# Decoder step on one core: head sums inside the attention, a gather in three parts, sample tokens twice on partitions, down weights split to 16 bits

## Chip, cores and metric

One core of a Trainium2 chip runs the whole program. The metric is the device time of one execution in microseconds; time before is the median of three runs. A profiled execution gives the trace.

## What is computed

One inference step of a two-layer decoder for a prompt group (256 tokens) and a sample group (8 sequences of 8 tokens), D = 1024, all in float32; T = 320 tokens in all.

```
layer 0: x += W_out_a [mLSTM heads | gated short conv] (rmsnorm(x))
layer 1: x += W_out_c [rms_norm per head(diff_attention(rope(q), rope(k), v)) * subln_g * (1 - lam_init)]
         (8 heads of 128; prompt causal, samples over a paged cache of 256 positions)
both:    x += W_mem_o mem_attention(rmsnorm(x))       (4 heads over 256 memory tokens)
         x += MoE(rmsnorm(x)): 4 groups of 8 experts, top 1 group, top 2 experts in it;
              y = sum_e gate_e * W_down_e( silu(W_gate_e x) * (W_up_e x) ),  d_ff = 256
end:     rmsnorm(x)
outputs also: new states, keys and values of the step
```

## The kernel before, in words

**Projections.** Weights arrive in units of 256 columns on SP's queue, in the order of `STREAM`. ACT makes the high float16 part (`split_hi`, L539), DVE the low part (`split_lo`, L546), and PE multiplies in three float16 products (`mm3`, L552 to L554). The low part of a unit releases its landing buffer, for which SP waits. Activations are kept with features on partitions, tokens on the free axis.

**Attention** (`attend_pe`, `attend_act`, `attend_dve`; kind "d" is the differential one of layer 1, "m0" and "m1" the memory ones). Eight iterations, one sample sequence each; in "d" each has also a prompt unit `u` (64 queries, four heads). Per iteration PE does scores, key transposes (L1406), weight transposes (`weights_t`, L1433; `unit_t`, L1485) and mixes (L1445, L1501), ACT the exponentials and copies (the last of a unit is L1570, into `xn`), DVE maxima and factors.

**Norm of the heads** (`subln_*`), when all units are done: ACT squares all of `xn` (L1818), PE sums with a matrix of ones (L1812), ACT takes logarithm and exponential in halves (L1822, L1823; each change of function loads a table), DVE scales (L1832). Then `input_act` and `input_dve` split `xn` in two halves, and `gemm_pe("out_c")` starts.

**Routing** (`memo_pe`, `route_*`). Router logits are computed with tokens on partitions in three tiles of 128, 128 and 64 tokens (L641), between the units of the memory output projection, the last set behind it, as are the token sums (L656). PE transposes the normalized tokens (L1847), ACT and DVE split them to `xnh` and `xnl`, DVE picks the experts, PE ranks the tokens (L1853 to L1858), and DVE builds `pk`, a 0/1 matrix from tokens to 704 slots sorted by expert (128 slots first, 576 later). The largest count of an expert, ready at L1940, goes to `roff`; `moe` loads it on each engine and branches: experts with at most 64 tokens take the body with one round, which is the one that runs here.

**Experts** (`moe_*`). PE gathers expert inputs into `xg` by products of `xnh` and `xnl` with `pk` (`gather_first`, L2007: six products for each of nine chunks; last the gates, L2015; then it transposes the positions, L2020). POOL copies 64 slots of each of the pair's two experts to `xe` (L2236, L2250). PE multiplies in float32 with the gate and up weights (`up`, L2048), two 64-row halves of the array for the two experts, followed by `weigh`, whose end releases the gate and up buffer (`gu_used`). After the first pair's `up` comes the gather of the other 576 slots in two halves (L2034, 108 products of 288 columns), with copies by ACT (L2167) and DVE (L2197). Step q is: `up(q)`, `weigh(q)`, `select(q)` (L2070), `combine(q-2)` (L2092), `down(q-1)` in two halves (L2112, float32) around `transpose_h(q)` (L2121). DVE makes the hidden values (L2214 to L2219), ACT and DVE split the result to `yh` and `yl` (L2171, L2204), and DVE's last step there releases the down buffer (`dw_used`). In layer 1, `seed` (L2081) adds x into the output banks before the second pair.

**SP's queue for the experts** (L430, L439) is written out by hand: pairs 0 and 1 with their down weights and pair 2's gate and up weights (there are two buffers of each, so pair g waits for the release of pair g-2), then for each p the gate and up weights of p+1 and the down weights of p. One pair is 4 MB of gate and up and 2 MB of down weights, 16 pairs a layer.

## Time and profile before

| | |
|---|---|
| median of three runs | 1442.78 us (1439.38 to 1445.84) |
| profiled execution | 1440.08 us, span 1438.8 us |
| granted TensorE clock, mean | 0.939 |
| PE busy | 1276.6 us, 89% |
| DVE / ACT / POOL busy | 582.3 / 413.9 / 143.6 us |
| read from HBM, written | 328.21 MB, 10.54 MB |
| experts' stages | about 485 to 745 us and 1160 to 1426 us |
| differential attention | about 862 to 950 us |

The span is from the first to the last instruction; the execution's own time has some 1.3 us more around it. A busy share is an average over stages with different limits, so a stage is read by its own rows. In the timeline a row gives the start, the duration, engine, line, operation, output and inputs, how many instructions are merged, and in brackets how long the engine was idle before and what ended that.

### The profile page before, as it was taken

Reading aid. Unit: us, or ns where it says so; the run is one execution under the profiler, and the core shown is the slowest. Engines: PE = TensorE matmul, PEld = TensorE weight load, DVE = VectorE, ACT = ScalarE, POOL = GpSimd, SP = SyncE. Lnnn points to the kernel's source line nnn. Section 1 sums busy time; section 2 is a strip of 40 time slices with the busy share of each in tenths; the row PEclk is TensorE's granted clock in tenths of the full one; section 3 lists DMA queues with packets and bytes.
Section 4 is the critical chain, followed back from the end, with each engine's and each line's share of the span. In section 5 each row is a group of like instructions: output and inputs, shape, how many; then the busy total and the mean of one; then the engine's idle time right before and its main releaser. Section 6 shows DMA issues by size and latency. Waiting matters only on the chain.

```text
span 1438.8 us, 20890 instructions
## 1 busy us (share of the span) xinstructions
PE 1276.6 (89%) x8470; PEld 793.9 (55%) x8470; DVE 582.3 (40%) x1152; ACT 413.9 (29%) x729; POOL 143.6 (10%) x189
## 2 busy tenths in 40 slices
PE   6799999989889799989989979958897979999995
PEld 5676688866656543333337757735664755333332
DVE  3655367655434522211244665425433452121212
ACT  3443323254332211111144224444432311111112
POOL 5100031110001110100000230000000101010100
PEclk9799998799998799999999989988998979999998
DMA  8464353357638069999963567302963624999992
GB/s 243 153 210 123 116 164 114 109 180 282 246 119 359 3 248 421 421 421 421 421 219 118 194 203 267 114 0 88 319 239 149 283 89 187 421 421 420 421 422 112
DMA packets 112826, 340.22 MB, mean 236 GB/s; under 512 B 7486, under 2 KB 75402, under 8 KB 84048
## 3 DMA queue, kind: packets, MB, share of 16 engines
q1 hardware_dynamic: 107296, 322.20, 59.5%
q0 software_dynamic: 4992, 15.47, 3.4%
q8 instruction: 69, 1.13, 0.3%
q10 hardware_dynamic: 432, 1.11, 0.2%
q14 instruction: 37, 0.30, 0.1%
HBM read 328.21 MB, written 10.54 MB: 235 GB/s over the span
## 4 chain that ended last, share of the span: by engine, by line
PE 66%; DMA 19%; DVE 7%; ACT 3%; issue 3%; SPq 1%; POOL 1%; POOLq 0%; ACTq 0%; DVEq 0%
DMA arena<-in_w_exp_up 15%; PE ps L2048 11%; PE ps L552 8%; PE ps L553 8%; PE ps L554 8%; PE ps L2112 2%; PE ps L1445 2%; PE ps L1501 2%; PE ps L2034 2%; PE ps L2092 2%; PE ps L1420 2%; PE ps L1406 1%; PE ps L1485 1%; DVE wl L546 1%; DMA stg<-in_w_mem_k 1%
## 5 line engine op out<-in xcount | busy, mean ns | idle before, releaser
L2048 PE MATMUL ps<-arena,mkv 128*64 128x512 f32 x1024 | 230.1, 601 | 26.8 <-DMA arena<-in_w_exp_up 21.7
L552 PE MATMUL ps<-bx,wh 128*128 128x320 f16 (+1 forms) x640 | 195.3, 305 | 38.9 <-DVE bx L777 15.5
L546 DVE SCALAR_TENSOR_TENSOR wl<-stg,wh 128x1024 f16<-128x1024 f32 x128 | 160.8, 1295 | 98.3 <-ACT wh L539 98.3
L553 PE MATMUL ps<-bx,wh 128*128 128x320 f16 (+1 forms) x640 | 195.2, 305 | 0.0
L554 PE MATMUL ps<-bx,wl 128*128 128x320 f16 (+1 forms) x640 | 195.0, 305 | 0.0
L539 ACT ACTIVATE wh<-stg 128x1024 f16<-128x1024 f32 x128 | 128.4, 1050 | 180.3 <-PE ps L554 158.1
L2048 PEld LDWEIGHTS ps<-arena,mkv 128*64 128x64 f32 x1024 | 82.1, 138 | 170.3 <-issue 164.8
L2204 DVE TENSOR_TENSOR arena<-ps,arena 128x512 f16<-128x512 f32 x64 | 44.1, 689 | 143.2 <-ACT arena L2171 92.4
L552 PEld LDWEIGHTS ps<-bx,wh 128*128 128x128 f16 x640 | 65.2, 102 | 65.5 <-issue 34.7
L552 PE MATMUL ps<-arena,wh 128*128 128x320 f16 x288 | 87.7, 304 | 3.7 <-DVE arena L1368 3.0
L2208 DVE COPY arena<-ps 128x1 f32<-128x1 f32 x32 | 5.1, 158 | 211.5 <-PE ps L2070 211.5
L554 PE MATMUL ps<-arena,wl 128*128 128x320 f16 x288 | 87.6, 304 | 0.0
L553 PE MATMUL ps<-arena,wh 128*128 128x320 f16 x288 | 87.6, 304 | 0.0
L2171 ACT CAST arena<-ps 128x512 f16<-128x512 f32 x64 | 37.5, 586 | 166.0 <-PE ps L2112 166.0
L2092 PE MATMUL ps<-arena,rstd 128*128 128x512 f16 (+1 forms) x384 | 78.9, 384 | 5.7 <-DVE arena L2204 5.7
L553 PEld LDWEIGHTS ps<-bx,wh 128*128 128x128 f16 x640 | 64.8, 101 | 24.5 <-issue 1.5
L554 PEld LDWEIGHTS ps<-bx,wl 128*128 128x128 f16 x640 | 64.9, 101 | 24.0
L2250 POOL COPY mkv<-bx 128x576 f32 x60 | 40.1, 671 | 375.5 <-PE ps L2070 316.9
L2176 ACT ACTIVATE mkv<-ps 128x256 f32<-128x256 f32 x30 | 11.5, 384 | 221.9 <-PE ps L2048 221.9
L1406 PE MATMUL ps<-cst,arena 128*128 128x128 f32 x384 | 57.3, 284 | 12.1 <-DVE arena L1580 7.7
L2112 PE MATMUL ps<-arena,mkv 128*64 128x512 f32 x256 | 61.5, 598 | 0.0
L2112 PE MATMUL ps<-stg,mkv 128*64 128x512 f32 x256 | 60.6, 597 | 0.0
(414 smaller groups left out, 1849.1 us busy)
## 6 DMA issues: line engine op xcount, KB each, us to landing
arena<-in_w_exp_gate SPq DMA_DIRECT2D x64, 1024.0 KB, 15.1
arena<-in_w_exp_up SPq DMA_DIRECT2D x64, 1024.0 KB, 17.2
arena<-in_w_exp_down SPq DMA_DIRECT2D x32, 1024.0 KB, 17.7
stg<-in_w_exp_down SPq DMA_DIRECT2D x32, 1024.0 KB, 17.6
arena<-in_cache_mem_k SPq DMA_DIRECT2D x16, 1024.0 KB, 7.1
arena<-in_cache_mem_v SPq DMA_DIRECT2D x16, 1024.0 KB, 5.2
stg<-in_w_in_a SPq DMA_DIRECT2D x28, 512.0 KB, 4.7
stg<-in_w_qkv_c SPq DMA_DIRECT2D x20, 512.0 KB, 4.3
```

The lines of the kernel that those rows point to most:

```text
L539: nc.scalar.mul(wh[:, s, c], src[:, c], WSCALE).then_inc(S["w_hi"], 1)
L546: nc.vector.scalar_tensor_tensor(wl[:, s, c], src[:, c], WSCALE, wh[:, s, c], ALU.mult, ALU.subtract).then_inc(S["w_lo"], 1)
L552: nc.tensor.matmul(out, wh[:, s, at:at + 128], hi, start=start, stop=False)
L553: nc.tensor.matmul(out, wh[:, s, at:at + 128], lo, start=False, stop=False)
L554: return nc.tensor.matmul(out, wl[:, s, at:at + 128], hi, start=False, stop=stop)
L1406: last = nc.tensor.transpose(ps[:, TB[f % 2], 256 * i + 128 * t:256 * i + 128 * t + 128], kpg[:, b % 2, t, at:at + 128], ident)
L2048: last = nc.tensor.matmul(ps[64 * j:64 * j + 64, UB, :], xe[:, q % 2, j, k, :], gu[:, g % 2, j, :, k, :], start=(k == 0), stop=(k == KD - ...
L2092: last = nc.tensor.matmul(out, csel[:, q % 3, 128 * i:128 * i + n], y[:, 512 * half:512 * half + 512], start=(first and y is yh), stop=(fi ...
L2112: last = nc.tensor.matmul(ps[64 * j:64 * j + 64, (Y0, Y1)[half], :], hT[:, q % 2, 128 * kk + 64 * j:128 * kk + 64 * j + 64], dws[g % 2][:, ...
L2171: nc.scalar.copy(yh[:, 512 * half:512 * half + 512], ps[:, (Y0, Y1)[half], :]).then_inc(M["y_hi"], 1)
L2204: V.tensor_tensor(yl[:, f], ps[:, (Y0, Y1)[half], :], yh[:, f], ALU.subtract).then_inc(M["y_lo"], 1)
L2250: nc.gpsimd.tensor_copy(xe[:, q % 2, j], xg[:, :, ds(at, CAP)]).then_inc(M["xe_ready"], 1)
```

## The change

Four parts:

1. **Head sums in the attention.** ACT squares each prompt unit when it is mixed, PE sums it in the next iteration in front of `weights_t`, DVE copies the sums out in front of `unit_factors`; the sample tokens' squares come with the last unit. Behind the attention are left the logarithms, then root, scaling, high and low part by chunk pairs; the first unit of `out_c` takes the pairs as they come.
2. **Sample tokens twice on partitions** (`per_token`). The third tile's 64 tokens stand in both halves of the 128 partitions, by two products each in logits, sums and transposes. The upper half of `xnh`'s third tile holds the low part, so that a gather needs five products and not six.
3. **Gather in three parts** of 128, 128 and 448 slots. The first (`first_pe`, `first_act`) stands in front of the branch on PE and ACT, with the gates and the position transposes. Then `up(0)`, the second part, three chunks of the third, `up(1)`, and the other six chunks. `seed` comes after the first step's down products.
4. **Down weights of pairs 2 to 14** (`HALVED`) are split by ACT and DVE to `dnh` and `dnl` (`halve`); three float16 products replace one in float32, and `hT` is split as well (`hTl`, for which `up(q+1)` waits). The down buffer is released when DVE has made the low part.

```diff
+    def per_token(out, x, rhs, i, **flags):
+        if i < 2:
+            return nc.tensor.matmul(out, x[:, 128 * i:128 * i + 128], rhs, skip_group_check=True, **flags)
+        for half in range(2):
+            last = nc.tensor.matmul(out[64 * half:64 * half + 64], x[:, NP:T], rhs, skip_group_check=True, **flags)
+        return last
...
@@ attend_pe @@
+        def head_sum(u):
+            pe.wait_ge(S["hsq_ready"], HA + u + 1)
+            pe.wait_ge(S["ppv_ev"], u0 + u + 1)
+            nc.tensor.matmul(ps[:, PVB, 256:512], ones[:], sqd[:, u % 2, :], start=True, stop=True,
+                             skip_group_check=True).then_inc(S["hsum_ready"], 1)
...
+            if c["diff"] and i:
+                head_sum(i - 1)
             weights_t(i)
...
@@ attend_act @@
+                if c["diff"] and u == 7:
+                    act.wait_ge(S["bpv_ev"], b0 + 8)
+                    nc.scalar.activation(sqs, xn[:, :, NP:T], ACT.Square).then_inc(S["hsq_ready"], 1)
                 act.wait_ge(S["ppv_ps"], u0 + u + 1)
+                if c["diff"]:
+                    if u >= 2:
+                        act.wait_ge(S["hsum_ready"], u)
+                    nc.scalar.activation(sqd[:, u % 2, :], ps[:, PVB, 0:256], ACT.Square).then_inc(S["hsq_ready"], 1)
...
@@ attend_dve @@
             weights(i)
+            if c["diff"] and i:
+                head_sums(i - 1)
...
@@ subln_act @@
-        nc.scalar.activation(sq[:], xn[:], ACT.Square).then_inc(S["hsq_ready"], 1)
-        act.wait_ge(S["hsum_ready"], 2)
-        for half in range(2):
-            h = slice(4 * half, 4 * half + 4)
-            link(nc.scalar.activation(sq[:, h], ps[:, h, 0:T], ACT.Ln, bias=epsc[:, 0:1], scale=1.0 / 128))
-            nc.scalar.activation(sq[:, h], sq[:, h], ACT.Exp, scale=-0.5).then_inc(S["hstd_ready"], 1)
+        act.wait_ge(S["hsum_ev"], 7)
+        log(slice(0, 4), slice(0, NP), hsum[:, 0:4, 0:NP])
+        log(slice(4, 8), slice(0, 192), hsum[:, 4:8, 0:192])
+        act.wait_ge(S["hsum_ready"], 9)
+        log(slice(0, 8), slice(NP, T), ps[:, 2, :].rearrange("p (h t) -> p h t", h=KD))
+        act.wait_ge(S["hsum_ready"], 10)
+        link(log(slice(4, 8), slice(192, NP), ps[:, 3, 0:256].rearrange("p (h t) -> p h t", h=4)))
+        root(0)
+        root(1)
+        high(0)
+        root(2)
+        high(1)
+        root(3)
+        high(2)
+        high(3)
...
@@ moe_pe @@
+    PARTS = ((xnh, 0), (xnl, 0), (xnh, 1), (xnl, 1), (xnh, 2))
+    RBANK = (0, 1, 6, 2, 3, 4)
+    HALVED = range(2, NPAIR - 1)
...
+            if rounds == 1 and q in HALVED:
+                for kk in range(2):
+                    pe.wait_ge(S["dn_lo"], 4 * (len(HALVED) * l + q - HALVED[0]) + 2 * half + kk + 1)
+                    for n, (h, w) in enumerate(((hTh, dnh), (hTh, dnl), (hTl, dnh))):
+                        for j in range(2):
+                            at = 128 * kk + 64 * j
+                            last = nc.tensor.matmul(ps[64 * j:64 * j + 64, (Y0, Y1)[half], :], h[:, q % 2, at:at + 64],
+                                                    w[:, j, kk, f], start=(kk == 0 and n == 0),
+                                                    stop=(kk == 1 and n == 2), skip_group_check=True)
...
         if rounds == 1:
             up(0)
             weigh(0)
-        gather(0, 18)
-        select(0)
-        transpose_h(0)
-        if l == 1:
-            seed()
+            gather_next()
+            gather_rest(0, 3)
+            select(0)
+            transpose_h(0)
+            up(1)
+            weigh(1)
+            gather_rest(3, 9)
...
@@ moe_act @@
+        def halve(q):
+            g = NPAIR * l + q
+            act.wait_ge(dw_in[g % 2], 32 * (g // 2 + 1))
+            if q == HALVED[0]:
+                act.wait_ge(S["xg_ps"], 15 * l + 15)
+            for half in range(2):
+                f = slice(512 * half, 512 * half + 512)
+                if q - 1 in HALVED:
+                    act.wait_ge(M["y_ps"], 2 * q - 1 + half)
+                for kk in range(2):
+                    nc.scalar.mul(dnh[:, :, kk, f], dws[g % 2][:, :, kk, f], WSCALE).then_inc(S["dn_hi"], 1)
...
         for q in range(last_step + 1):
+            if rounds == 1 and q - 1 in HALVED:
+                halve(q - 1)
+            gate_half(q)
...
@@ pe_memory, act_memory @@
         route_pe(pe, l)
+        first_pe(pe, l)
         moe(pe, l, moe_pe)
```

## Rows read from the trace of the kernel before

**Rows 1.** The page, chain that ended last: shares by engine.

```profile
PE 66%; DMA 19%; DVE 7%; ACT 3%; issue 3%; SPq 1%; POOL 1%; POOLq 0%; ACTq 0%; DVEq 0%
DMA arena<-in_w_exp_up 15%; PE ps L2048 11%; PE ps L552 8%; PE ps L553 8%; PE ps L554 8%; PE ps L2112 2%; PE ps L1445 2%; PE ps L1501 2%; PE ps L2034 2%; PE ps L2092 2%; PE ps L1420 2%; PE ps L1406 1%; PE ps L1485 1%; DVE wl L546 1%; DMA stg<-in_w_mem_k 1%
```

**Rows 2.** Stretches: length, busy of PE, PEld, DVE, ACT, POOL; clock, DMA share, GB/s.

```profile
600.00:700.00 100.00, 92.50 (x462) 35.56 (x464) 19.45 (x47) 11.37 (x25) 9.36 (x14) 1.00 1.01 421
```

**Rows 3.** Timeline of PE, one step of the expert stage.

```profile
544.63 7.04 PE L2048 MATMUL ps<-arena,mkv 128*64 128x512 f32 x32
...
551.83 2.47 PE L2092 MATMUL ps<-arena,rstd 128*128 128x512 f16 x12
554.13 1.88 PE L2112 MATMUL ps<-arena,mkv 128*64 128x512 f32 x8
...
558.15 7.04 PE L2048 MATMUL ps<-arena,mkv 128*64 128x512 f32 x32
```

**Rows 4.** Timeline of SP's queue: pair 3's weights, layer 0, layer 1.

```profile
527.02 0.33 SPq L430 DMA_DIRECT2D arena<-in_w_exp_gate  x1
...
1208.09 0.33 SPq L430 DMA_DIRECT2D arena<-in_w_exp_gate  x1
```

**Rows 5.** Timeline around the branch and the first pairs, both layers; L2034: chain of waits.

```profile
480.66 0.14 DVE L1940 TENSOR_SCALAR roff<-arena 1x1 int32<-1x1 f32 x1
...
483.63 4.03 DVE L1959 SCALAR_TENSOR_TENSOR wl<-ps,rtok,wh 128x512 f16<-128x512 f32 x6
485.51 2.72 PE L2007 MATMUL ps<-arena,wh 128*128 128x128 f16 x24 [6.12 <-issue]
...
491.00 0.54 PE L2020 MATMUL ps<-cst,arena 128*32 128x128 f32 x3
...
493.92 8.78 PE L2048 MATMUL ps<-arena,mkv 128*64 128x512 f32 x32 [2.38 <-POOL mkv L2236]
...
502.76 13.35 PE ps L2034 x108
...
519.84 7.09 PE L2048 MATMUL ps<-arena,mkv 128*64 128x512 f32 x32 [0.51 <-POOL mkv L2250]
...
1169.20 8.79 PE L2048 MATMUL ps<-arena,mkv 128*64 128x512 f32 x32 [2.11 <-POOL mkv L2236]
...
1194.61 6.20 PE L2081 MATMUL ps<-cst,xT 128*128 128x128 f32 x45
```

**Rows 6.** Timeline, end of the differential attention and norm of the heads.

```profile
929.24 0.88 PE L1433 MATMUL ps<-arena,bx 128*128 128x64 f32 x6 [1.03 <-DVE arena L1591]
...
949.61 0.37 ACT L1570 COPY bx<-ps 128x256 f32<-128x256 f32 x1 [2.09 <-PE ps L1501]
...
952.43 1.28 ACT L1822 ACT_TABLE_LOAD   x1
952.46 7.47 PE L1812 MATMUL ps<-arena,ones 128*128 128x320 f32 x16 [2.89 <-ACT arena L1818]
...
964.00 1.55 DVE L1832 SCALAR_TENSOR_TENSOR bx<-bx,lams,arena 128x1280 f32<-128x1280 f32 x1 [16.48 <-ACT arena L1823]
...
975.45 0.44 PE L552 MATMUL ps<-bx,wh 128*128 128x320 f16 x1 [15.51 <-DVE bx L777]
```

**Rows 7.** Stretches as in rows 2, start of the output projection.

```profile
975.00:1001.00 26.00, 25.55 (x176) 17.89 (x177) 13.38 (x15) 10.61 (x15) 2.22 (x2) 0.93 0.27 84
```

**Rows 8.** Timeline of the routing in layer 0.

```profile
450.08 1.57 PE L641 MATMUL ps<-wrt,bx 128*128 128x36 f32 x12
...
473.24 4.69 PE L1847 MATMUL ps<-cst,bx 128*128 128x128 f32 x24
...
478.28 0.26 DVE L1922 TENSOR_TENSOR arena<-arena 128x96 bf16<-128x96 f32 x1
```

**Rows 9.** The page, groups: line, shapes, count, busy, mean ns, idle before.

```profile
L546 DVE SCALAR_TENSOR_TENSOR wl<-stg,wh 128x1024 f16<-128x1024 f32 x128 | 160.8, 1295 | 98.3 <-ACT wh L539 98.3
...
L539 ACT ACTIVATE wh<-stg 128x1024 f16<-128x1024 f32 x128 | 128.4, 1050 | 180.3 <-PE ps L554 158.1
```

More of the change, by code:

```diff
@@ L655, in memo_pe @@
             for c in (0, 1, 6, 7):
[L656 to L657 removed]
+                last = per_token(ps[:, 7, i:i + 1], sq[:, c, :], ones[:, 0:1], i, start=(c == 0 and i == 0),
+                                 stop=(c == 7))
         last.then_inc(S["sum_ready"], 1)
@@ new lines, in subln_pe @@
+        nc.tensor.matmul(ps[:, 2, :], ones[:], sqs.rearrange("p h t -> p (h t)"), start=True, stop=True
+                         ).then_inc(S["hsum_ready"], 1)
+        pe.wait_ge(S["hsq_ready"], HA + 9)
+        nc.tensor.matmul(ps[:, 3, 0:256], ones[:], sqd[:, 1, :], start=True, stop=True
+                         ).then_inc(S["hsum_ready"], 1)
+        u0, base = UNIT["out_c"][0], IN["out_c"][0]
+        pe.wait_ge(S["w_ev"], u0)
+        for p in range(4):
+            if p % 2 == 0:
+                pe.wait_ge(S["w_lo"], u0 * 2 + p // 2 + 1)
+            pe.wait_ge(S["in_lo"], base + p + 1)
+            last = unit_mm(0, T, xh, xl, ks=(2 * p, 2 * p + 1))
@@ new lines, in subln_pe, with log, root, high @@
+        last.then_inc(S["w_used"], 1)
+        gemm_pe(pe, "out_c", first=1)
+    def subln_act(act, link):
+        def log(h, t, src):
+            return nc.scalar.activation(hsum[:, h, t], src, ACT.Ln, bias=epsc[:, 0:1], scale=1.0 / 128)
+        def root(p):
+            k = slice(2 * p, 2 * p + 2)
+            nc.scalar.activation(hsum[:, k], hsum[:, k], ACT.Exp, scale=-0.5).then_inc(S["hstd_ready"], 1)
+        def high(p):
+            k = slice(2 * p, 2 * p + 2)
+            act.wait_ge(S["y_ready"], p + 2)
+            nc.scalar.copy(xh[:, k], xn[:, k]).then_inc(S["in_hi"], 1)
+        act.wait_ge(S["hsum_ev"], 7)
[13 more added lines that the diff above has]
+        high(3)
@@ L1837, in build @@
+        scaled(0)
+        scaled(1)
+        low(0)
+        scaled(2)
+        low(1)
+        scaled(3)
+        low(2)
+        low(3)
     NFIT = ROUNDS * NE
@@ new lines, in gather_rest @@
+        def gather_rest(k0, k1):
+            for k in range(k0, k1):
+                if k < 2:
+                    pe.wait_ge(S["xg_act"], 10 * l + k + 2)
+                elif k in (3, 4, 5):
+                    pe.wait_ge(S["xg_dve"] if k == 4 else S["xg_act"], 5 * l + 1 if k == 4 else 10 * l + 5)
+                elif k >= 6:
+                    pe.wait_ge(S["xg_dve"] if k % 2 else S["xg_act"], 5 * l + 2 if k % 2 else 10 * l + 6 + (k - 6) // 2)
+                for n, (x, i) in enumerate(PARTS):
+                    last = nc.tensor.matmul(ps[:, RBANK[k % 6], 0:SR], x[:, i, k, :], pk[:, i, S1:NSLOT],
+                                            start=(n == 0), stop=(n == 4))
@@ L2147, in moe_pe @@
             down(q - 1, 1)
+            if q == 1 and l == 1:
+                seed()
         combine(last_step - 1)
@@ L2151, in moe_pe, with first_act @@
         combine(last_step)
+    def first_act(act, l):
+        for b in range(3):
+            act.wait_ge(S["xg_ps"], 15 * l + b + 1)
+            dst = xg[:, 4 * b:4 * b + 4, 0:S0] if b < 2 else xg[:, KD, 0:S0]
+            src = ps[:, FIRST[b], :].rearrange("p (k c) -> p k c", k=4) if b < 2 else ps[:, FIRST[b], 0:S0]
+            nc.scalar.copy(dst, src).then_inc(S["xg_act"], 1)
     def moe_act(act, l, rounds):
```

372 lines of the change are left out of this document (213 added, 159 removed).

## The prediction

> **What bounds the kernel now.** I read the chain that ended last first. Products on PE hold most of it, and the one transfer in it is the experts' gate and up weights with 15% of the span [rows 1]. The question is where that transfer decides, so the stretch table came next: between 600 and 700 us the DMA engines move 421 GB/s, busy share 1.01 [rows 2]. A pair of experts brings 4 MB of gate and up and 2 MB of down weights, 6.29 MB, so 14.9 us at that rate. PE's own step is shorter, 13.5 us from one pair's up products to the next (544.63 to 558.15) [rows 3]. Both expert stages are therefore bound by the transfer, once it runs without a gap. What sets their end is when that gapless run begins. SP's queue says when: the up weights of pair 3 are issued at 527.02 and 1208.09 [rows 4], and from there all follows at 14.9 us a pair. The first up products start at 493.92 and 1169.2 [rows 5]. I call this point U: pair 3 is released at U+33.1 in layer 0 and U+38.9 in layer 1.
>
> The second place is the norm between the differential attention and its output projection. The last mix ends at 949.6, and the projection's first product starts at 975.45 [rows 6]: 25.8 us in which ACT, PE and DVE take turns.
>
> **1. Head sums in the attention.** Removed: one Square over 2560 elements, eight f32 sums (7.47 us), the four passes of logarithm and exponential with four table loads of 1.28 us, and the wait of all casts for both scalings (1.55 us each) [rows 6]. What is left behind the last mix, with durations scaled by elements: Square and copy 0.8, load 1.3, four logarithms (2560 elements, at the splits' 1.05 us per 1024 [rows 9], with starts) 2.8, load 1.3, first root 0.7, DVE's scaling 0.8, ACT's cast 0.65, DVE's remainder 0.75; sum 9.3 after 949.6, so the first product at 958.9. The other three chunk pairs come 1.4 to 1.6 us apart, and PE's 12 products for each take as long. The projection ran 176 products in 25.55 us at a granted clock of 0.93 [rows 7]: 0.135 us each at full speed and 1.8 us lost at the start. Before, its first unit of 48 products ends at 975.4+6.5+1.8=983.7. Now the first pair runs at half clock (3.2 us), the others at 1.6: 958.9+3.2+4.9=967.0. That is 16.7 us earlier; the units behind it follow their splits as before, and so does the wait for the memory output weights.
>
> Added in each of eight iterations: an f32 sum over 256 columns (0.53 us for 320, so 0.43), a Square on ACT (0.37), a DVE copy (0.4). The sum stands in front of the product that waits 1.03 us for DVE [rows 6], which covers it; the Square lies between the mix and the next exponentials, where ACT is idle. The DVE copy stands in front of the factors that the next weight transposes wait for, with about 0.2 us of cover. If all were covered, nothing; if all were serial, 1.2 us an iteration, 8.4 in seven. I take 1.6, since the longest of the three is inside a shown wait. Net 15.1.
>
> **2. The gather.** After U: up products of pair 0, 8.8 us [rows 5]. Then 45 products of 128 columns; 24 took 2.72 us at half clock [rows 5], so 2.5 in all at full speed (5 at the other). Then 15 of 448 columns, 0.19 each by the 2.30 us of 12 products [rows 3]: 2.8. Select, gate and transposes: before, 17.1 us between the end of up products and pair 1's (502.7 to 519.84) hold 13.4 of gather [rows 5], leaving 3.7; a last eviction is no longer waited for, so 3.3. Pair 1 starts at U+17.4 and releases pair 3's weights at U+24.6, 8.5 us sooner. The other 30 gather products (5.7), an eviction (0.7), pair 0's down products with the transposes (4.0 by 554.13 to 558.15 [rows 3]) and pair 2's up products (7.1) put the release of pair 4 at U+42.3. In between the queue runs dry for some us: pair 3's transfer ends at about U+36. So the gain is not 8.5: before, pair 4's turn came at U+33.1+14.9=U+48.0, now it comes at U+42.3, 5.7 sooner. In layer 1 the seed, 6.2 us for 45 records at a mixed clock [rows 5], moves from before pair 1 to before pair 2, and runs at about 4.8 there: U+47.1 against U+53.8, 6.7.
>
> **3. U itself moves.** Sample tokens twice on partitions means two 64-wide f32 products for one. Router logits: 12 records take 1.57 us [rows 8]; four more per call, three calls inside a PE-bound projection: 1.3. The sums and the last call: 8 records at 0.1 and 4 at 0.18: 1.6. The last eight of 24 transposes (4.69 us for all [rows 8]) become 32 records. No row has 64-wide f32 records of 128 columns; a quarter of the up products' 0.22 us is 0.054, the seed's average record is 0.138, and I take 0.08: 2.6 us. They would end at 480.6, half a us behind the expert mask (478.54 [rows 8] plus 1.6): 0.6 (0 to 2.5). DVE's route loses a memset and four split operations: minus 0.5. Sum 3.0.
>
> Then the branch. The count is ready at 480.80, and PE's first product behind its branch starts at 485.51, 6.1 idle, "issue", though DVE had its last operand at 483.6 and went on to the low parts [rows 5]: 4.7 us for load, compare and jump. It lies before the first gather now, where DVE's work on slots covers most of it. The change puts the branch behind the first gather and the position transposes, which end at 491.54 and would end at 494.5. So U goes from 493.92 to 498.7 (4.7, less 0.5 for a sequencer that runs ahead): 4.8 later. Expert inputs would be there sooner: DVE's low parts end at 487.66 plus 3, eight products 0.9, ACT's copy 0.6, POOL's load and copies 2.2: 494.3. If the jump were free, U moves 0.6.
>
> The Trainium skill (Runtime: NRT & Kernel Launch, Instruction fetch mechanics) says that a taken branch to code outside the fetched window stalls for a DMA fetch. By it the jump costs PE wherever it stands in the program, which speaks against the move: 4.2 us a layer that a free jump would not take. By that rule the sum is 1425, without it 1416.6. The idle time named "issue" agrees with it.
>
> Net: layer 0 5.7-4.8=0.9, layer 1 6.7-4.8=1.9.
>
> **4. Down weights split.** Before, 8 f32 products a pair: 4.0 us with transposes 0.4. After, 24 f16 products of 64 columns' width. In the combine, 8 wide ones and 4 of half width take 2.30 us [rows 3]; 8 at 0.213 leave 0.6, 0.15 each, so half-width ones overlap in twos. 24 take 2.6 to 3.6, I say 2.8: PE saves 0.8 a pair, and the step goes to about 12.8. Added: ACT four splits a pair (1.05 each), DVE four (1.30 each) [rows 9], DVE's low part of the hidden rows 0.4. DVE is then busy for 8.7 of 14.9 us, ACT 6.1. The splits wait for down weights, and ACT's tanh of the next pair is queued behind them: with the weights 5 us after the up weights, tanh comes at 9.6, the second half's split ends at 13.4 and the next up products may start at 14.6, just under 14.9. A step that misses this starts late once, and takes from no transfer, as weights are released 11 us before their turn. Worth nothing: the transfer hides it. The last pair isn't split, and combine(14) falls within 0.3 us of where it was.
>
> **Sum.** 15.1+0.9+1.9=17.9: the profiled 1438.8 (1440.08 with what lies around it) becomes 1420.9. It ran 2.7 below the median of 1442.78; from the median: 1424.9, say 1425.
>
> **Rivals.**
> - *The jump is hidden after all* (code fetched while PE waits for DVE). Against: "issue" in both layers. 4.2 us a layer: 1416.6. Chance 0.17.
> - *The attention pays in full*: the copy, sum and Square in series, 8.4 instead of 1.6: 1431.8. For it: the factors stand right behind the copy. Against: the 1.03 us wait in front of the sum. 0.15.
> - *Half-width f16 products don't overlap*: 24 at 0.213 are 5.1, step 15.3, 0.4 over the transfer in 26 steps: 1435. Against: the combine. 0.07.
> - *Slower: PE becomes the bound of the expert stage.* The same place, with each half-width product's weight load (0.05) uncovered too: 6.3 us, step 16.5, 1.6 in 26 steps: 1466. It decides from a step of 15.9, where the 17.9 and 7.2 us are used up. 0.06.
> - *The gather gives nothing and the transposes in the route run at 0.138*: 2.5 us more a layer and no earlier release: 1438. 0.05.
>
> The split does take effect: it stands in the one-round branch, and the 13.5 us steps are those of one round a pair.
>
> **How the numbers follow.** Forecast 0.50, its own range 1420 to 1431. 0.5% is 7.2 us, about what a measurement of this kernel can tell: faster below 1435.6. Faster: 0.50+0.17+0.15 and half of the third rival, 0.84; same 0.09; slower 0.07. The range 1414 to 1436 leaves out the slow case, the last and part of the noise.
>
> **What would show it.** The first projection product behind the attention 9 us after the last mix; iterations there up to 0.3 us longer; PE idle some 4.7 us with "issue" between position transposes and first up products; pair 3's weights issued 25 us after those, pair 4's at 42 and 47; 14.9 us a pair with 421 GB/s; a DVE row of splits at 1.3 us with no wait of PE on it. I would be wrong if the stretches fall below 421 GB/s, if the attention's iterations grow by a us, or if the jump isn't there.

## The result and the profile after

| | before | after |
|---|---|---|
| median | 1441.72 us (1439.38 to 1445.84, 4 runs) | 1422.27 us (1418.38 to 1424.52, 4 runs) |
| profiled execution, its span | 1440.08, 1438.8 | 1424.52, 1423.2 |
| PE, DVE, ACT busy | 1276.6, 582.3, 413.9 | 1260.6, 713.2, 511.3 |

The ratio is 0.9859 (95%: 0.9827 to 0.9891). It is faster, by 19 us where 17.9 were worked out, and 1422.3 lies inside the range and 3 us under the forecast. A second timing of the same kernel gave 1421.31 and a ratio of 0.9880 (0.9850 to 0.9911).

Where it went shows when the span is cut at instructions that both kernels have: the issue of the experts' first weights, the first staged loads of the next projection behind them, the loads of the second and third cached values, the loads of the next memory weights. In us, from one cut to the next:

| stretch | before | after | again | gain |
|---|---|---|---|---|
| start to experts' first weights, layer 0 | 430.33 | 432.94 | 424.24 | |
| layer 0's experts, to the projection's loads | 311.26 | 311.60 | 309.62 | -0.3, 1.6 |
| projection, to the cached values | 120.26 | 119.42 | 118.14 | |
| attention, norm, first output units | 124.46 | 108.01 | 108.10 | 16.4 |
| memory attention | 119.13 | 119.16 | 119.14 | 0 |
| layer 1's experts, to the end | 333.36 | 332.07 | 331.96 | 1.3, 1.4 |

So, by the stages of these profiles, one of the four parts carries the change: the head sums. The first stretch has the same code in all kernels and still differs by 8.7 us between two executions of one; that is the size of what one execution can't tell.

The end of the differential attention and its norm, timeline of after (start, length, engine, line, out<-in; in brackets the idle time before and who ended it):

```profile
949.45 2.00 PE L1522 MATMUL ps<-bx,arena 128*128 128x64 f32 x16 [0.45 <-ACT bx L1590]
...
952.15 1.28 ACT L1865 ACT_TABLE_LOAD   x1
...
953.45 1.97 ACT L1865 ACTIVATE mkv<-mkv,epsc 128x1024 f32<-128x1024 f32 x2
955.33 1.03 ACT L1865 ACTIVATE mkv<-ps,epsc 128x512 f32<-128x512 f32 x2
...
957.66 1.36 ACT L1869 ACTIVATE mkv<-mkv 128x640 f32<-128x640 f32 x2
958.54 1.68 DVE L1902 SCALAR_TENSOR_TENSOR bx<-bx,lams,mkv 128x640 f32<-128x640 f32 x2 [9.16 <-ACT mkv L1869]
959.46 0.72 ACT L1874 CAST bx<-bx 128x640 f16<-128x640 f32 x1 [0.43 <-DVE bx L1902]
...
961.19 0.43 PE L558 MATMUL ps<-bx,wh 128*128 128x320 f16 x1 [8.40 <-DVE bx L1908]
```

It answers to [rows 6]. The last mix ends at 951.45, the projection's first product starts at 961.19: 9.7 us, where before had 25.8. Behind the mix stand ACT's square and copy (0.7 us), a table load, four logarithms of 3.0 us in all, a second load, the first root, DVE's scaling and ACT's cast. PE's idle time falls from 15.51 to 8.40.

Then the branch and the first pairs. Timeline of after: DVE, PE and POOL in layer 0 (count ready, first gather, its gate part, position transposes, expert inputs, the up products of pairs 0 and 1), last row layer 1:

```profile
483.25 0.14 DVE L2021 TENSOR_SCALAR roff<-arena 1x1 int32<-1x1 f32 x1
...
486.61 1.87 PE L2083 MATMUL ps<-arena,wh 128*128 128x128 f16 x16 [4.41 <-DVE arena L2032]
...
494.00 0.29 PE L2099 MATMUL ps<-arena,wh 128*128 128x128 f16 x1 [2.76 <-DVE roff L2059]
...
494.50 0.85 PE L2104 MATMUL ps<-cst,arena 128*32 128x128 f32 x3
...
495.19 0.84 POOL L2429 COPY mkv<-bx 128x64 f32 x2 [1.73 <-ACT bx L2284]
...
499.16 9.29 PE L2151 MATMUL ps<-arena,mkv 128*64 128x512 f32 x32 [3.81 <-issue]
...
517.00 8.78 PE L2151 MATMUL ps<-arena,mkv 128*64 128x512 f32 x32 [0.51 <-issue]
...
1157.15 3.68 PE L2151 MATMUL ps<-arena,mkv 128*64 128x512 f32 x8 [3.43 <-issue]
```

It answers to [rows 5]. POOL has the experts' inputs ready at 496.0, DVE nothing that PE needs, and PE stands still from 495.4 to 499.16 with "issue": 3.81 us, 3.43 in layer 1. Pair 1's up products take 8.78 us, before 7.09. The releases, timeline of SP's queue in after, pair 3 and pair 4 in layer 0, then in layer 1:

```profile
525.88 0.33 SPq L436 DMA_DIRECT2D arena<-in_w_exp_gate  x1
...
543.46 0.33 SPq L436 DMA_DIRECT2D arena<-in_w_exp_gate  x1
...
1184.26 0.33 SPq L436 DMA_DIRECT2D arena<-in_w_exp_gate  x1
...
1207.12 0.33 SPq L436 DMA_DIRECT2D arena<-in_w_exp_gate  x1
```

From the experts' first weights (432.94 and 1091.13) these are 92.9, 110.5, 93.1 and 116.0; before, pair 3 came at 96.7 and 102.7 [rows 4]. The stretches of after (length, busy of PE, PEld, DVE, ACT and POOL, clock, DMA share, GB/s):

```profile
505.00:560.00 55.00, 52.36 (x297) 22.04 (x294) 15.93 (x32) 12.11 (x22) 7.21 (x10) 0.97 0.76 307
600.00:700.00 100.00, 89.43 (x512) 36.76 (x512) 51.21 (x79) 38.25 (x55) 8.47 (x12) 0.98 1.01 421
```

The second answers to [rows 2]: 421 GB/s as before, and the clock of PE at 0.98 instead of 1.00. Between 505 and 560 the queue runs dry in two places (share 0.76), which is where a sooner release can gain anything.

A step of the expert stage, timeline of PE in after: the first down products, the transposes behind the first half's twelve, the last down products, the next up products:

```profile
641.87 0.38 PE L2222 MATMUL ps<-wh,mkv 128*64 128x512 f16 x2
...
643.26 0.51 PE L2237 MATMUL ps<-cst,mkv 128*128 128x128 f32 x2
...
645.09 0.38 PE L2222 MATMUL ps<-wh,mkv 128*64 128x512 f16 x2
647.24 1.08 PE L2151 MATMUL ps<-arena,mkv 128*64 128x512 f32 x4 [1.77 <-DMA arena<-in_w_exp_up]
```

Twelve products of half width take 1.39 us (641.87 to 643.26), 24 take 2.8; the whole answers to [rows 3]. The next up products wait 1.77 us for their weights, not for the splits. The splits themselves (groups by line; count, busy, mean ns, idle before), one of two rows each:

```profile
L2222 PE MATMUL ps<-wh,mkv 128*64 128x512 f16 x416 | 74.3, 383 | 1.6 <-DVE wl L2367 0.2
L2367 DVE SCALAR_TENSOR_TENSOR wl<-arena,wh 128x1024 f16<-128x1024 f32 x56 | 67.6, 1248 | 63.9 <-ACT wh L2315 63.9
...
L2315 ACT ACTIVATE wh<-arena 128x1024 f16<-128x1024 f32 x56 | 54.5, 1045 | 59.0 <-DMA arena<-in_w_exp_down 59.0
```

DVE's splits take 1.25 us, ACT's 1.05; PE waits 0.2 us for them in 416 products.

### The profile page after: what moved, and what is told of

Its sections match the earlier page's. It is cut to its first block and busy times, and to the rows that moved or that the text cites. A ratio compares the mean times of both kernels' runs of the same rounds, so it can differ in the third digit from the quotient of the medians.

```text
span 1423.2 us, 21723 instructions
## 1 busy us (share of the span) xinstructions
PE 1260.6 (89%) x8724; PEld 791.9 (56%) x8724; DVE 713.2 (50%) x1273; ACT 511.3 (36%) x839; POOL 141.6 (10%) x185
## 5 line engine op out<-in xcount | busy, mean ns | idle before, releaser
L2151 PE MATMUL ps<-arena,mkv 128*64 128x512 f32 x1024 | 240.3, 623 | 36.6 <-DMA arena<-in_w_exp_up 27.6
L552 DVE SCALAR_TENSOR_TENSOR wl<-stg,wh 128x1024 f16<-128x1024 f32 x128 | 160.9, 1296 | 96.1 <-ACT wh L545 95.9
L545 ACT ACTIVATE wh<-stg 128x1024 f16<-128x1024 f32 x128 | 128.4, 1050 | 177.5 <-PE ps L560 154.5
L2151 PEld LDWEIGHTS ps<-arena,mkv 128*64 128x64 f32 x1024 | 87.4, 143 | 175.6 <-issue 175.2
L2367 DVE SCALAR_TENSOR_TENSOR wl<-arena,wh 128x1024 f16<-128x1024 f32 x56 | 67.6, 1248 | 63.9 <-ACT wh L2315 63.9
L2367 DVE SCALAR_TENSOR_TENSOR wl<-stg,wh 128x1024 f16<-128x1024 f32 x48 | 58.2, 1253 | 56.3 <-ACT wh L2315 56.3
L2320 ACT ACTIVATE arena<-ps 128x512 f16<-128x512 f32 x64 | 38.2, 597 | 125.7 <-PE ps L2222 99.4
L2443 POOL COPY mkv<-bx 128x576 f32 x60 | 43.0, 729 | 375.2 <-PE ps L2173 291.3
L2222 PE MATMUL ps<-wh,mkv 128*64 128x512 f16 x416 | 74.3, 383 | 1.6 <-DVE wl L2367 0.2
L2315 ACT ACTIVATE wh<-arena 128x1024 f16<-128x1024 f32 x56 | 54.5, 1045 | 59.0 <-DMA arena<-in_w_exp_down 59.0
L2315 ACT ACTIVATE wh<-stg 128x1024 f16<-128x1024 f32 x48 | 46.7, 1045 | 52.1 <-DMA stg<-in_w_exp_down 52.1
```

The source lines that it names most:

```text
L545: nc.scalar.mul(wh[:, s, c], src[:, c], WSCALE).then_inc(S["w_hi"], 1)
L552: nc.vector.scalar_tensor_tensor(wl[:, s, c], src[:, c], WSCALE, wh[:, s, c], ALU.mult, ALU.subtract).then_inc(S["w_lo"], 1)
L2151: last = nc.tensor.matmul(ps[64 * j:64 * j + 64, UB, :], xe[:, q % 2, j, k, :], gu[:, g % 2, j, :, k, :], start=(k == 0), stop=(k == KD - ...
L2222: last = nc.tensor.matmul(ps[64 * j:64 * j + 64, (Y0, Y1)[half], :], h[:, q % 2, at:at + 64], w[:, j, kk, f], start=(kk == 0 and n == 0), ...
L2315: nc.scalar.mul(dnh[:, :, kk, f], dws[g % 2][:, :, kk, f], WSCALE).then_inc(S["dn_hi"], 1)
L2367: last = V.scalar_tensor_tensor(dnl[:, :, kk, f], dws[g % 2][:, :, kk, f], WSCALE, dnh[:, :, kk, f], ALU.mult, ALU.subtract)
```

## The experiments

Twelve timings of nine kernels. "After" is the changed kernel, and each ratio is against the kernel before on the same chip. "Last pair" means pair 15 of a layer, "the stretch" in experiments 1 and 8 the one from the cached values to the next memory weights.

**1. Head sums alone** (two timings)

Edit: the kernel before, with the parts of the diff on the attention, its norm and the output projection. They brought along the shorter clearing by POOL (the sample tile's rows aren't all set to zero), so that part of the computation is left out; POOL's busy time falls from 143.6 to 138.8 us.

> The kernel before, with the head sums alone added (the sums in the attention's iterations and the norm in four chunk pairs); gather, routing and expert stages are those of before. Theory (what the two traces show): from the first cache load of the differential attention to the first load of the next memory weights the changed kernel is 16.4 us shorter, and its iterations are not longer; so 16.4 under the kernel before, 1425.3. The prediction's own term was 15.1 (1426.6). Rival (the attention pays in full for copy, sum and Square): 8.3, so 1433.4. Rival (the gain comes from the expert stages and the norm's gain is eaten by the transfer of the next weights): under 5, above 1436.

> The kernel before with the head sums alone, again: its first timing gave 13.2 us, of which the trace found 16 in the attention and 2.75 lost in layer 0's experts, whose code is that of before (pair 1's up products took 9.59 us there, at the lower clock level for longer). Expected: attention and norm 108.0 to 108.7 us from the cached values' loads to the next projection's loads (124.5 before), and 15.5 to 16.5 us under the kernel before if the 2.75 were one execution's. Rival (the loss belongs to this kernel): 13.2 again.

Measured: 1428.66 us, ratio 0.9903 (0.9882 to 0.9924), and 1430.69, ratio 0.9924 (0.9895 to 0.9953). The stretch of attention and norm is 108.70 and 108.54 us. Layer 1's experts take 333.1 and 333.2, as before. So the stretch gives 15.8 to 15.9 us in both profiles; the whole kernel gives 13.2 and 9.4 by its medians, 7 to 17 by the intervals. Of the 12 executions of the second timing five take 1420 to 1426 us (mean clock 0.944 to 0.948) and seven 1431 to 1435 (0.934 to 0.937). Both expected times (16.4, then 15.5 to 16.5 under the kernel before) were missed, and in the second timing the rival's 13.2 as well. The 16 are shown for the stretch; what takes some of it back in most executions goes with a lower clock, and its cause is open. The rival of 8.3 is out by the stretch.

**2. No pair split**

```
-    HALVED = range(2, NPAIR - 1)
+    HALVED = range(0)
```

> The changed kernel with no pair's down weights split (f32 down products in all 16 pairs). Theory (transfer hides it): PE's steps go back from 12.96 to 13.5 us where PE is ahead of the transfer, and stay at 14.9 where it isn't; at the end of each layer the next to last combine comes 0.6 us later; the up products of the last pairs no longer start at the lower of the two clock levels (8.78 against 7.09 us, once at the end of layer 0), which gives 1.7 back. Sum -0.5, so 1422, within 1.5 of the changed kernel. Rival A (the shorter step carries the gather's gain): some 5 us longer, 1427. Rival B (the splits cost clock or queue time in the steps): 3 or more us shorter, under 1419.

Measured: 1425.53 us, ratio 0.9884 (0.9862 to 0.9906). Releases of pairs 3 and 4 at 92.8 and 110.4, as in after, then steps of 13.5 us until the transfer takes over; layer 0's experts 310.5, layer 1's 333.05 (after 332.0). The end of layer 1 is 1.0 later, where pair 14's down products are f32 again. The time lies outside the expected 1.5 us around 1422, but its interval overlaps those of after, so the stages have to tell. By them the split is hidden by the transfer, as predicted; its 131 us on DVE and 99 on ACT (busy time, after less this kernel) buy 1 us at most, and in layer 0 they can cost more than they buy (part 4 of the next section). That is a piece of rival B.

**3. No branch on PE**

```
-        moe(pe, l, moe_pe)
+        moe_pe(pe, l, 1)
```

> The changed kernel, and PE runs the block for one round a pair without loading the count and without the branch (it leaves out the block for two rounds on PE; the other engines still branch). Theory (the idle time in front of the first up products is the branch): its 3.81 and 3.43 us vanish but for some 0.2, all later releases move with it, and the time falls by 7 us to 1415; with the prediction's 4.2 a layer by 8.4 to 1414. Rival (what PE waits for there is the experts' input or the positions, and the transfer decides anyway): PE waits for POOL or DVE instead, time 1422, unchanged within 1.5.

Measured: 1413.51 us, ratio 0.9777 (0.9749 to 0.9805). Timeline of PE in layer 1: position transposes, up products of pairs 0 and 1:

```profile
1151.80 0.85 PE L2104 MATMUL ps<-cst,arena 128*32 128x128 f32 x3
1152.58 7.96 PE L2151 MATMUL ps<-arena,mkv 128*64 128x512 f32 x32
...
1169.10 7.09 PE L2151 MATMUL ps<-arena,mkv 128*64 128x512 f32 x32 [0.51 <-issue]
```

The idle time is gone, and the up products start 3.9 and 3.7 us sooner after the experts' first weights (62.3 in both layers for 66.2 and 66.0). In layer 1 they also take 7.96 and 7.09 us instead of 9.68 and 8.78, so there the stop of 3.4 us goes with a loss of clock as well. In layer 0 they stay at 9.51 and 8.79, so it isn't the stop alone. Pair 4's release is 3.7 and 7.1 sooner, layer 1's experts take 324.4 us for 332.0. As expected, the idle time named "issue" was the branch. The edit takes out the load of the count, the compare and the jump together; which of the three costs the time isn't shown.

**4. The branch in front of the first gather** (two timings)

```
         route_pe(pe, l)
-        first_pe(pe, l)
         moe(pe, l, moe_pe)
...
+        first_pe(pe, l)
         if rounds == 1:
             up(0)
```

> The changed kernel with PE's branch back in front of the first gather; nothing else is moved. Theory (a branch costs 4.7 us from the count wherever it stands, and DVE's slots cover it in front of the gather): the first gather starts 1.5 us later (count ready at 483.4, plus 4.7), its gate part still waits for DVE until 494.0, so the first up products follow the position transposes directly, near 495.5 instead of 499.2: 3.6 us a layer, time 1415. Rival (the jump is no cost of its own; the block is then further from the wait): no change, 1422. Rival (first gather later delays the experts' input as much): 1.5 a layer longer, 1425.

> The changed kernel with PE's branch in front of the first gather, again, beside the next one on one chip. The first time it ran 13.6 us under the changed kernel, and its profiled execution was 9.2 us ahead of it when the experts' first weights were issued, in code that is the same. Theory (the branch is worth its releases: pair 4 at 104.2 and 109.6 us from the first weights, instead of 110.5 and 116.0): 6.3 in layer 0 and 6.4 in layer 1, some 11 to 13 in all by the stages, near 1410. Rival (most of it was the early stages' luck): 5 under the changed kernel, 1416.

Measured: 1408.66 us, ratio 0.9764 (0.9739 to 0.9789), and 1412.07, ratio 0.9800 (0.9761 to 0.9838). Timeline of this kernel in layer 0: DVE's count and its last slots, PE's first gather, gate part, first up products:

```profile
474.16 0.14 DVE L2021 TENSOR_SCALAR roff<-arena 1x1 int32<-1x1 f32 x1
...
477.02 0.35 DVE L2032 SCALAR_TENSOR_TENSOR arena<-mkv,arena 128x128 f16<-128x128 f32 x1
...
479.29 1.86 PE L2083 MATMUL ps<-arena,wh 128*128 128x128 f16 x16 [6.17 <-issue]
...
484.47 0.23 PE L2099 MATMUL ps<-arena,wh 128*128 128x128 f16 x1 [0.76 <-DVE roff L2059]
...
486.01 1.51 PE L2151 MATMUL ps<-arena,mkv 128*64 128x512 f32 x6 [0.71 <-POOL mkv L2427]
```

Count ready at 474.30, first gather at 479.29: 5.0 us, where before had 4.7 in this place [rows 5]. DVE's last slots end at 477.4, so 1.9 us are not covered, but the gate part waits for DVE anyway and absorbs them: only 0.76 us of wait are left there, where after had 2.76. The up products then start when POOL has the inputs, 62.2 and 63.0 after the first weights, as without any branch. Pair 4's release moves from 110.5 and 116.0 to 104.2 and 109.6 (second profile 105.4 and 111.3); the two expert stages take 304.8 and 324.9 us (304.8 and 326.7). It beats both kernels. Its profiled execution of the first timing was also 9.2 us ahead of after before the experts began, in unchanged code; the second timing, 9 us under after, lies between what its theory (near 1410) and its rival (1416) said. In the first profile the releases of pair 4 move by 6.3 and 6.4 us, more than the 4.0 and 3.0 by which the up products start sooner: pair 0's take 7.09 and 7.98 us, in after 9.29 and 9.68.

**5. All rest parts of the gather in front of pair 1**

```
-            gather_rest(0, 3)
+            gather_rest(0, 9)
             select(0)
             transpose_h(0)
             up(1)
             weigh(1)
-            gather_rest(3, 9)
```

(ACT's and DVE's evictions follow the same order.)

> The changed kernel with all nine rest parts of the gather in front of pair 1's up products, not three in front and six behind; the engines that evict them follow. Theory (the transfer takes each pair up when it is released and when the one before is through): pair 3's weights are released 5.7 us later in both layers, pair 4's are not. Layer 0: pair 3 at 531.6, so pair 4's turn comes at 546.5 instead of 543.5, 3.0 lost. Layer 1: pair 3 at 1190, turn at 1204.9, still ahead of pair 4's release at 1207.1, nothing lost. 3.0 in all, 1425. The prediction's rival that the gather gives nothing: its 12.4 us of gather gain come back but for the seed's part, 1434. Third (the order of the rest parts doesn't matter at all): 1422.

Measured: 1418.58 us, ratio 0.9839 (0.9810 to 0.9867). The expected loss of 3.0 us and the rival of 12 are out: it is 2.7 us under after on the same chip, which is within the noise. Its expert stages take 310.94 and 330.36 us (after 311.60 and 332.07, 309.62 and 331.96). Layer 1 gains 1.6. Layer 0 loses 1.3 against the profile of after that ran its last pair at the same clock level, the one with 309.62 (part 4 of the next section); in the other the last pair took 1.7 more. Timeline of PE in layer 0: select, transposes, pair 1's up products, transposes, pair 2's:

```profile
519.59 0.33 PE L2173 MATMUL ps<-rstd,identb 128*64 128x320 f16 x2
521.68 0.51 PE L2237 MATMUL ps<-cst,mkv 128*128 128x128 f32 x2 [1.77 <-DVE mkv L2397]
522.70 7.09 PE L2151 MATMUL ps<-arena,mkv 128*64 128x512 f32 x32 [0.51 <-POOL mkv L2438]
...
534.34 1.89 PE L2151 MATMUL ps<-arena,mkv 128*64 128x512 f32 x8
```

Pair 3's release is only 3.8 us later (96.7 and 97.0), and pair 4's is 2.2 and 2.4 sooner (108.3 and 113.6). Pair 1's up products take 7.09 us here and 8.78 in after. In both they follow a wait of 1.77 us and one of 0.51; what differs is that PE ran 11 us of gather ahead of them here, and 5.4 there. That this is the cause isn't shown: in layer 1 of experiment 3 the same up products take 7.09 behind the short gather, and in layer 0 of head sums alone 9.59 behind the long gather of before. The wait for an eviction behind the last rest part (0.37 in after's second profile) is gone too.

**6. Seed behind pair 2's up products** (layer 1)

```
+            if q == 2 and l == 1:
+                seed()
             if q >= 2:
                 combine(q - 2)
...
-            if q == 1 and l == 1:
-                seed()
```

> The changed kernel with layer 1's seed behind pair 2's up products instead of in front of them. Theory: pair 4's weights are released 4.8 us sooner (16 us behind pair 3's instead of 22.9), but the release of pair 5 stays where it is, and the transfer of pair 4 is through by then; the gap moves to pair 5 and only 1.4 us are gained: 1421. Rival (the stream runs without a gap from pair 4 on, whenever that is): 4.8, so 1417.5. Rival (the seed is on the path in either place): nothing.

Measured: 1420.95 us, ratio 0.9890 (0.9854 to 0.9925); after on the same chip 1421.31. Pair 4 is released at 110.5 (after 116.0), pair 5 at 129.3 (129.5), and layer 1's experts take 331.07 us for 331.96: 0.9 gained, where 1.4 were expected. The gap moved to pair 5; the rival of 4.8 is out. The last pair's up products of layer 1 take 8.78 us here and 7.09 in after.

**7. Both moves** (the edits of experiments 4 and 6 together, two timings)

> Both moves in one: PE's branch in front of the first gather, and layer 1's seed behind pair 2's up products. Theory: the first up products 3.0 to 4.0 us sooner in each layer, and all releases with them, 7 in all, and 1.4 from the seed: 8.4 under the changed kernel of this call, near 1414, with the expert stages at 308 and 323.5. Rival (the earlier run of the branch in front gained by its early stages alone, where its code is the same): within 2 of the changed kernel.

> PE's branch in front of the first gather and layer 1's seed behind pair 2's up products, again. Theory (a layer ends a fixed time after the latest of its releases, less 14.9 for each pair behind pair 4): pair 5, released at 123.3, now sets layer 1, which puts it 1.2 ahead of the kernel with the branch alone (109.6 against 123.3 less 14.9). So 1.2 under that kernel, within noise. Rival (the seed's place costs pair 5 what pair 4 gains): equal. Rival (the seed's move does harm): more than 3 above it, as in the first timings, on two chips.

Measured: 1416.45 us, ratio 0.9831 (0.9802 to 0.9860), and 1413.12, ratio 0.9822 (0.9787 to 0.9856). The first lies 4.9 us under after where 8.4 were expected. On one chip the kernel with the branch alone has 1412.07 and this one 1413.12, so equal, where 1.2 less were expected; the 3 us and more of harm did not come back. Layer 1's experts take 325.2 and 328.2 us, with the branch alone 324.9 and 326.7. In both profiles the last pair's up products of layer 1 take 8.78 us, with the branch alone 7.09, so the 1.2 us that the move of the seed gives D at most are spent there.

**8. DVE's copy of the head sums twice**

```
+            V.tensor_copy(spare, ps[:, PVB, 256:512])
             V.tensor_copy(hsum[...], ps[:, PVB, 256:512]...)
```

> The changed kernel with DVE's copy of the head sums made twice in each of the attention's iterations (the second into an area of its own). The prediction put 0.2 us of cover behind the one copy of 0.41 and charged 1.6 us for seven iterations; the trace shows them no longer than before. Theory (DVE has 0.3 us left behind the copy, by its last factor at 933.56 and PE's next product at 933.88): the second copy, 0.41 us, reaches past it by 0.1 in seven iterations, so the attention's stretch goes from 108.0 to 108.8. Rival (the copy is on the path): 0.41 in seven, 110.9. Rival (there is more cover than the trace lets see): 108.0.

Measured: 1423.80 us, ratio 0.9886 (0.9840 to 0.9933); the stretch of attention and norm 108.01 us, as in after to the hundredth: of the three expectations the last holds, more cover. Timeline: both copies, the last factor, PE's next weight transposes:

```profile
932.54 0.41 DVE L1653 COPY mkv<-ps 128x256 f32<-128x256 f32 x1
...
932.87 0.42 DVE L1654 COPY mkv<-ps 128x256 f32<-128x256 f32 x1
...
933.67 0.42 DVE L1680 TENSOR_TENSOR arena<-cst,arena 128x256 f32<-128x256 f32 x1
...
934.15 1.10 PE L1505 MATMUL ps<-arena 128*128 128x64 f32 x8
```

The iteration starts 0.23 us later here. The factors end at 934.09 instead of 933.56, so 0.3 later by the second copy, and PE takes them up at 934.15, 0.04 later than it would have. The first copy had a cover of its own on DVE, the wait for ACT's last exponential in front of the factors. Timeline of DVE, the first instruction of the factors, in before and in after:

```profile
930.77 0.18 DVE L1638 RECIPROCAL arena<-arena 128x4 f32<-128x4 f32 x1 [0.26 <-ACT arena L1546]
```

```profile
932.65 0.18 DVE L1674 RECIPROCAL arena<-arena 128x4 f32<-128x4 f32 x1
```

Both stand 1.53 us behind the start of the weight transposes (929.24 and 931.12), so the first copy delays the factors by nothing; it fills the 0.26.

**9. The changed kernel again**

> The changed kernel once more, on the chip of the next three, since its stages ahead of the experts differ by up to 11 us between kernels whose code there is the same (the experts' first weights are issued at 432.9 here, at 423.8 to 435.2 in four other kernels). Expected 1422, with the expert stages at 311.6 us from their first weights to the next projection's loads and 332.1 from there to the end in layer 1, each within 1.5. Rival (the difference between programs is one of the placement of code): the same program then gives 432.9 within 0.5 at the first weights.

Measured: 1421.31 us (1412.47 to 1429.18). The experts' first weights are issued at 424.24, not at 432.94, by the same program: the difference belongs to the execution, and the rival (placement of code) is out. The expert stages take 309.62 and 331.96 us; the second is as expected, the first 2.0 shorter, 0.5 outside. The stretch from 260 to 305 us, first of after, then of this execution:

```profile
260.00:305.00 45.00, 41.30 (x293) 35.10 (x292) 28.59 (x42) 19.46 (x22) 6.30 (x8) 0.87 0.49 158
```

```profile
260.00:305.00 45.00, 41.30 (x315) 33.72 (x314) 32.01 (x46) 22.90 (x27) 5.90 (x7) 0.96 0.48 156
```

PE is as busy, at a granted clock of 0.87 and 0.96.

## Why the prediction was right

**What decides an expert stage.** The prediction took pair 4's turn, the later of its own release and pair 3's release plus 14.9 us. Extended to every pair (D: the latest of all releases from pair 3 on, less 14.9 us for each pair behind pair 4), it accounts for every kernel within 1 us: layer 0's experts end 199.2 to 201.3 us after D in 14 profiles, layer 1's 215.3 to 217.1, while D itself runs from 104.2 to 114.3 and from 108.4 to 117.6. The rule took this form in the course of the runs, not before them.

| kernel | pair 3, 4 in layer 0 | D | pair 3, 4 in layer 1 | D |
|---|---|---|---|---|
| before | 96.7, 107.9 | 111.6 | 102.7, 113.9 | 117.6 |
| after | 92.9, 110.5 | 110.5 | 93.1, 116.0 | 116.0 |
| rest parts first | 96.7, 108.3 | 111.6 | 97.0, 113.6 | 113.6 |
| seed late | 93.5, 111.1 | 111.1 | 92.9, 110.5 | 114.4 (pair 5) |
| no branch | 89.3, 106.9 | 106.9 | 86.0, 108.9 | 108.9 |
| branch first | 86.6, 104.2 | 104.2 | 86.7, 109.6 | 109.6 |

**1. Head sums.** Right, and sized a little low: 9.7 us from the last mix to the first product where 9.3 were worked out, and 16.4 net for the stretch, not 15.1. The error is the charge of 1.6 us for the iterations. It was worked out from 0.2 us of cover behind DVE's copy and left out the 0.26 us for which DVE itself waits in front of the factors: the copy fills them, and even a second copy, which moves the factors by 0.3, costs PE 0.04. The eight terms behind the last mix add up to 9.1, not 9.3; measured are 9.7. The rival "the attention pays in full" is refuted by the same row.

**2. The gather.** The mechanism (pair 3 no longer decides, pair 4 does) is what the releases show, but two terms were off. Pair 0's up products were put at 8.8 us and took 9.29 and 9.68, pair 1's at 7.1 and took 8.78, so pair 3's release came at U+26.7 and U+27.1, not U+24.6, and pair 4's at U+44.3 and U+50.0, not 42.3 and 47.1. (The terms written down for pair 4 add up to 42.1; and what rows 4 show of pair 3 is the issue of its gate weights, the up weights follow 0.4 us later.) And the gain was credited to the three parts around pair 1 in both layers. Putting all rest parts back in front of pair 1 makes pair 3 decide again in layer 0 (D 111.6 for 110.5) and costs 1.3 us there at equal clock; in layer 1 it gives 1.6, since pair 4 decides there and comes 2.4 sooner when pair 1's up products run at the full clock. So the three parts earn what they were meant to in layer 0 alone, and in layer 1 they cost.

**3. U itself moves.** Predicted 4.8 later in each layer; measured 2.6 and 2.3 (66.2 and 66.0 from the first weights, before 63.6 and 63.8). The branch was right: 3.81 and 3.43 us idle with "issue" where 4.2 were expected, gone with the branch. By the Trainium skill (Runtime: NRT & Kernel Launch, Instruction fetch mechanics) a taken branch out of the fetched window waits for a DMA fetch; experiments 3 and 4 agree with it, 5.0 us from count to first product, and add that the wait can lie under another engine's work. That the time is such a fetch, no run shows. Nor does one show the 0.5 us that the sum takes off by itself; the idle time behind the transposes is 3.8 and 3.4 us instead of the 4.2 that are left of 4.7. What was off is the sum of the route, 3.0: the position transposes end only 1.2 later (62.4 for 61.2 from the first weights), since the 32 records of 64 columns took 2.05 us and not 2.6, and the rest was hidden.

The errors of 2 and 3 cancel, and that is luck: 2.2 and 2.5 us sooner at U, 2.0 and 2.9 later from there to pair 4. Layer 0 should give 0.9, D moved by 1.1 and the stage by -0.3 in one profile and 1.6 in the other; layer 1 should give 1.9, D moved by 1.6 and the stage by 1.3 and 1.4.

**4. Down weights split.** Right in its terms: 24 half-width products 2.8 us, the step 12.96 where PE is ahead (12.8 predicted), 14.9 behind it, no wait. Not foreseen: PE now waits 1.75 us for weights and not 1.18, and in some steps starts the up products at the lower clock, 8.78 us. In the middle that is hidden, at the last pair it isn't. Last pair's up products in layer 0, first of after, then of its second profile:

```profile
721.82 8.78 PE L2151 MATMUL ps<-arena,mkv 128*64 128x512 f32 x32 [1.75 <-DMA arena<-in_w_exp_up]
```

```profile
712.54 7.09 PE L2151 MATMUL ps<-arena,mkv 128*64 128x512 f32 x32 [1.72 <-DMA arena<-in_w_exp_up]
```

That is why the two profiles differ by 2.0 us in this stage (311.60 and 309.62). With split down weights the last pair takes 8.78 us in six of ten profiles in layer 0 and in three of ten in layer 1 (the three with the seed late); without the split, in none of eight stages. Waits of 1.7 to 1.8 us for weights stand in front of both levels, so the wait doesn't decide by itself, and the cause is open. With this sorted out D fits layer 0 to some 0.4 us either way: the stage ends 200.6 to 201.3 us after D at 8.78, 199.2 to 200.1 at 7.09 (199.2 to 199.4 of them with the split, so it gives some 0.5). In layer 1, 1.8 us of spread are left (217.1 without the split, 216.8 with all rest parts first, both at 7.09), unexplained. At the end of layer 1 the splits do enter the chain that ended last (start, length, what):

```profile
1369.95 20.89 DMA arena<-in_w_exp_down
...
1390.87 3.90 ACT wh L2315 x4
...
1396.01 2.28 DVE wl L2367 x2
...
1398.33 0.86 PE ps L2222 x6
...
1400.59 2.47 PE ps L2195 x12
```

The down weights of pair 14 land at 1390.85, ACT and DVE split them (3.9 and 2.3 us) while PE has pair 15's up products, and the combine comes 14.6 us after those began, 15.2 before. So even there it gains 0.6, where the prediction had nothing (within 0.3).

**The sum.** 16.4 by the stretch, 1.1 and 1.6 by D, 19.1 against 17.9; by the lengths of the stages 17.4 in the first profile and 19.4 in the second; the medians say 19.4 and, the second time, 18.4. The forecast was 2.7 us over the result: 1.1 because it starts from 1442.78, where four runs have 1441.72, and 1.3 by the attention's charge. The rivals' chances fell as they should: the jump is real (0.17), the attention doesn't pay (0.15), half-width products overlap (0.07), PE doesn't bound the stage (0.06). Of the last one (0.05), that the gather gives nothing, the first half came true in part: the three parts around pair 1 gain in layer 0 and lose in layer 1. The prices of three rivals were wrong by their own terms: products that don't overlap make a step of 15.1, not 15.3, so 1430; with uncovered weight loads it is 16.3, not 16.5; and the last one, 12.4 us of releases and 5.0 of transposes given back, comes to 1442, not 1438. None of them took place. The chances for "faster" add up to 0.855 where 0.84 stands. Not settled: head sums alone gave 9 and 13 us by the medians though their stretch gave 16, so the medians leave 6 to 9 us to the other three parts, for which the releases show 3. On one chip the kernel without the split lies 3.1 us under head sums alone, on another the one with the copy twice 6.9 under; most of this is within the intervals.

## What to carry to other kernels

Where a transfer bounds a stage, list when each piece is released and take the latest, less the pieces behind it: only that release is worth moving, and moving an earlier one beyond it buys nothing and can cost what it displaces. Put a run-time branch where the engine already waits for another one; most of the 5 us from the count to the next product lie under that wait here, and moved behind it they left PE idle for 3.4 to 3.8. Count reductions that stand in a chain of three engines first: spreading them over the loop ahead cost nothing here and gave nearly all of the gain that the stages show.

## What the hardware showed unexpectedly

The lower clock level follows short stops of PE unevenly. The same attention code, with the same waits, ran its last iteration at full clock in after and at the lower one in the kernel with the branch in front, in both of its profiles. Timeline of PE in that kernel:

```profile
929.26 0.88 PE L1446 MATMUL ps<-arena,bx 128*128 128x64 f32 x6 [1.42 <-DVE arena L1621]
930.59 1.93 PE L1458 MATMUL ps<-arena,bx 128*32 128x256 f32 x24 [0.45 <-DVE bx L1631]
932.45 3.68 PE L1504 MATMUL ps<-arena 128*128 128x64 f32 x16
...
936.80 3.68 PE L1522 MATMUL ps<-bx,arena 128*128 128x64 f32 x16 [0.25 <-ACT bx L1590]
```

The weight transposes and the mix take 3.68 us each, in after 2.00. The waits ahead of them, 1.42 and 0.45 us, are those of after. It costs 5.4 us (113.6 and 113.3 for 108.0), so this kernel could be faster still. It doesn't hang on the branch alone: the kernel with branch and seed moved runs this iteration at 2.00 in both of its profiles, behind the same two waits. Why the clock falls there was not tried.

The mean granted clock of an execution goes roughly with its time: 17 executions of the kernel before run from 1432.0 us at 0.944 to 1446.9 at 0.934.
